# A 32-column projection on TensorE: three rounded passes in one corner of the array, or plain 32-bit products in four quarters of its columns

## What is computed

```python
D_MODEL = 1024; SEQ = 512; N_SSD_HEADS = 32; CHUNK = 128
...
zxbcdt = u @ w_in                       # u: (512, 1024), normed tokens
z, xbc, dt = jnp.split(zxbcdt, [D_INNER, D_INNER + D_XBC], axis=-1)   # dt: (512, 32)
xbc = jax.nn.silu(causal_depthwise_conv(xbc, conv_w, conv_b))
...
dt = jax.nn.softplus(dt + dt_bias)
a = -jnp.exp(a_log)
y = ssd_chunked(xh, dt, a, bm, cm)      # decays are exp of running sums of dt * a
```

## Time and profile before

| | |
|---|---|
| median of 3 runs | 1150.98 us (1150.7 to 1151.34) |
| profiled execution, its own time | 1151.16 us |
| its span | 1149.4 us |
| mean granted TensorE clock | 0.999 |
| TensorE (PE) busy | 1141.1 us, 99% of the span |
| VectorE (DVE) busy | 684.4 us, 60% |
| ScalarE (ACT) busy | 523.9 us, 46% |
| GpSimd (POOL) busy | 32.8 us, 3% |
| DMA queue of SyncE (q1) | 32.1% of 16 engines' span |

### The profile page before, as it was taken

One profiled execution on the slowest core, in us unless ns is written; L12 is line 12 of the kernel. 1 busy time (PEld: TensorE's weight loads), 2 busy tenths in 40 slices (PEclk: granted clock), 3 DMA queues, 4 the chain that ended last, 5 costly groups with the idle time before them and its releaser, 6 DMA issues.

```text
span 1149.4 us, 14668 instructions
## 1 busy us (share of the span) xinstructions
PE 1141.1 (99%) x5734; PEld 956.9 (83%) x5734; DVE 684.4 (60%) x783; ACT 523.9 (46%) x614; POOL 32.8 (3%) x87
## 2 busy tenths in 40 slices
PE   9999999999999999999999999999999999999998
PEld 8888888888788898888888888899888888888886
DVE  5678778888943865565555412487655565562124
ACT  5667676767523644444344211465444344342213
POOL 6000001000000000000000000000000000000000
PEclk9999999999999999999999999999999999999999
DMA  8243444443222323332322332512222323323321
GB/s 271 75 130 129 128 129 129 128 129 129 74 94 90 110 75 117 102 104 80 108 94 88 110 110 92 183 37 74 92 90 93 109 79 103 109 76 111 106 74 74
DMA packets 85246, 121.74 MB, mean 106 GB/s; under 512 B 4167, under 2 KB 71215, under 8 KB 85200
## 3 DMA queue, kind: packets, MB, share of 16 engines
q1 hardware_dynamic: 85018, 121.02, 32.1%
q10 hardware_dynamic: 182, 0.07, 0.0%
HBM read 118.92 MB, written 2.16 MB: 105 GB/s over the span
## 4 chain that ended last, share of the span: by engine, by line
PE 97%; DVE 2%; ACT 0%; issue 0%; POOL 0%; DVEq 0%; POOLq 0%; ACTq 0%
PE bank L994 28%; PE bank L300 18%; PE bank L302 18%; PE bank L301 18%; PE bank L497 6%; PE bank L777 2%; PE bank L786 1%; PE bank L414 1%; PE bank L709 1%; PE bank L736 1%; PE bank L1170 0%; DVE w_lo L270 0%; PE bank L764 0%; PE bank L437 0%; PE bank L432 0%; PE bank L1185 0%
## 5 line engine op out<-in xcount | busy, mean ns | idle before, releaser
L300 PE MATMUL bank<-h_hi,w_hi 128*128 128x512 f32 x928 | 364.1, 392 | 0.0
L302 PE MATMUL bank<-h_hi,w_lo 128*128 128x512 f32 x928 | 361.3, 389 | 0.0
L301 PE MATMUL bank<-h_lo,w_hi 128*128 128x512 f32 x928 | 361.1, 389 | 0.0
L270 DVE TENSOR_TENSOR w_lo<-raw,w_hi 128x2048 fp32r<-128x2048 f32 x90 | 206.2, 2291 | 219.7 <-ACT w_hi L265 219.7
L516 DVE SCALAR_TENSOR_TENSOR tmp<-bank,par,tmp 128x511 f32<-128x511 f32 (+2 forms) x248 | 184.7, 747 | 135.3 <-ACT tmp L507 122.4
L265 ACT ACTIVATE w_hi<-raw 128x2048 fp32r<-128x2048 f32 x90 | 171.5, 1906 | 152.5 <-PE bank L994 152.3
L302 PEld LDWEIGHTS bank<-h_hi,w_lo 128*128 128x128 f32 x928 | 174.2, 188 | 36.6
L301 PEld LDWEIGHTS bank<-h_lo,w_hi 128*128 128x128 f32 x928 | 174.3, 188 | 36.3 <-issue 0.7
L300 PEld LDWEIGHTS bank<-h_hi,w_hi 128*128 128x128 f32 x928 | 174.2, 188 | 36.4 <-issue 0.7
L507 ACT ACTIVATE tmp<-bank,par 128x512 f32<-128x512 f32 x112 | 86.3, 775 | 229.4 <-PE bank L302 209.5
L994 PE MATMUL bank<-w_hi,act_hi 128*128 128x512 f32 x348 | 107.2, 389 | 0.0
(11 more groups left out here) (193 smaller groups left out, 1035.9 us busy)
## 6 DMA issues: line engine op xcount, KB each, us to landing
raw<-in_ffn_w_up SPq DMA_DIRECT2D x44, 1024.0 KB, 5.1
raw<-in_ffn_w_down SPq DMA_DIRECT2D x22, 1024.0 KB, 5.0
raw<-in_ssd_w_in SPq DMA_DIRECT2D x19, 1024.0 KB, 5.5
decay<-ac_dram SPq DMA_DIRECT2D x16, 512.0 KB, 4.3
raw<-in_ssd_w_out SPq DMA_DIRECT2D x8, 1024.0 KB, 4.9
from_start<-ac_dram SPq DMA_DIRECT2D x32, 128.0 KB, 4.0
xres<-in_x SPq DMA_DIRECT2D x4, 512.0 KB, 5.7
result<-xres SPq DMA_DIRECT2D x3, 512.0 KB, 2.6
```

The lines of the kernel that those rows point to most:

```text
L270: dve.tensor_tensor(lo[:], raw[n % 2][:], hi[:].bitcast(F32), ALU.subtract).then_inc(lo_ready, 1)
L300: pe.matmul(dst, wh, xh, start=first, stop=False, **kw)
L301: pe.matmul(dst, wh, xl, start=False, stop=False, **kw)
L302: return pe.matmul(dst, wl, xh, start=False, stop=last, **kw)
```

## The change

The weights of the projection are no longer split. Each of the 8 contraction blocks `k` gives two plain 32-bit products, one with `h_hi` and one with `h_lo`, both read as fp32. Block `k` goes to quarter `k % 4` of the array's columns, and so to 32 of the 128 partitions of bank 7: two blocks in each quarter. The result is four partial sums stacked on 128 partitions. ScalarE copies all 128 rows. Where a 32 by 32 identity turned each chunk, a product with `fold` (128 by 32, four identities on top of each other) now turns it and adds the four partial sums at once. `fold` is built by GpSimd with three additions of slices of the identity, behind the masks that TensorE waits for at the start and ahead of the pooling windows.

```diff
-            wdt_hi = sb("wdt_hi", [P, DB, HEADS], F32R, scope=scope)
-            wdt_lo = sb("wdt_lo", [P, DB, HEADS], F32R, scope=scope)
+        fold = sb("fold", [P, HEADS])
...
         def dt_feat_act(act):
             act.wait_ge(dt_mm, 1)
-            act.activation(sq[0:HEADS, :], bank[0:HEADS, 7, :], ACT.Copy).then_inc(dt_feat_ready, 1)
+            act.activation(sq[:, :], bank[:, 7, :], ACT.Copy).then_inc(dt_feat_ready, 1)
...
-        def dt_split_act(act):
-            act.wait_ge(wdt_in, 16)
-            act.activation(wdt_hi[:], wdt_raw[:], ACT.Copy).then_inc(wdt_hi_ready, 1)
-
-        def dt_split_dve(dve):
-            dve.wait_ge(wdt_hi_ready, 1)
-            dve.tensor_tensor(wdt_lo[:], wdt_raw[:], wdt_hi[:].bitcast(F32), ALU.subtract).then_inc(wdt_ready, 1)
+        QUARTERS = P // HEADS
 
         def dt_product_pe(pe):
-            pe.wait_ge(wdt_ready, 1)
-            for k in range(DB):
-                mm = three_passes(pe, bank[0:HEADS, 7, :], wdt_hi[:, k, :], wdt_lo[:, k, :], h_hi[:, k, :],
-                                  h_lo[:, k, :], k == 0, k == DB - 1)
+            pe.wait_ge(wdt_in, 16)
+            for r in range(DB // QUARTERS):
+                for turn, part in enumerate((h_hi, h_lo)):
+                    for q in range(QUARTERS):
+                        k = r * QUARTERS + q
+                        mm = pe.matmul(bank[q * HEADS:(q + 1) * HEADS, 7, :], wdt_raw[:, k, :], part[:, k, :].bitcast(F32),
+                                       start=r == 0 and turn == 0, stop=r == DB // QUARTERS - 1 and turn == 1,
+                                       tile_position=(0, q * HEADS))
             mm.then_inc(dt_mm, 1)
 
         def dt_transpose_pe(pe):
             pe.wait_ge(dt_feat_ready, 1)
+            pe.wait_ge(fold_ready, 1)
             for c in range(NCH):
-                mm = pe.transpose(bank[:, 7, c * HEADS:(c + 1) * HEADS], sq[0:HEADS, cs(c)], ident[0:HEADS, 0:HEADS])
+                mm = pe.matmul(bank[:, 7, c * HEADS:(c + 1) * HEADS], sq[:, cs(c)], fold[:, :], start=True, stop=True)
             mm.then_inc(dt_T, 1)
...
             pool.wait_ge(consts, 4)
+            step(pool.tensor_tensor(fold[:, :], ident[:, 0:HEADS], ident[:, HEADS:2 * HEADS], ALU.add))
+            step(pool.tensor_tensor(fold[:, :], fold[:, :], ident[:, 2 * HEADS:3 * HEADS], ALU.add))
+            pool.tensor_tensor(fold[:, :], fold[:, :], ident[:, 3 * HEADS:], ALU.add).then_inc(fold_ready, 1)
...
-            dt_split_act(act)
...
-            dt_split_dve(dve)
```

More of the change, by code:

```diff
@@ L195, in hybrid_trunk @@
         x_sq, x_rms, x_rr, xn_ready = sem("x_sq"), sem("x_rms"), sem("x_rr"), sem("xn_ready")
+        fold_ready = sem("fold_ready")
         pre_spread, pre_kept, xn_half = sem("pre_spread"), sem("pre_kept"), sem("xn_half")
@@ L200, in hybrid_trunk @@
                                                                 sem("half_scaled"), sem("half_out"))
-        wdt_in, wdt_hi_ready, wdt_ready = sem("wdt_in"), sem("wdt_hi_ready"), sem("wdt_ready")
+        wdt_in = sem("wdt_in")
         dt_feat_ready, dt_T = sem("dt_feat_ready"), sem("dt_T")
```

## The result

The changed kernel takes 1157.05 us (1156.89 to 1157.78, 6 runs) against 1150.89 us before (6 runs): ratio 1.0057, 95% interval 1.0047 to 1.0067. It is 6.2 us slower, where 1.4 us faster was forecast. The profiled span is 1155.4 us, for 1149.4.

What follows compares the result with a forecast made beforehand. TensorE was taken to bound the kernel, busy 1141.1 of 1149.4 us. Product -1.76 and transposes +0.34 gave -1.4 us, from 1151.16 to 1149.7, set to 1149.6 for the runs' median; range 1148.8 to 1150.2.

Steps and rivals of the forecast that it cites:

- the product: The dt product on TensorE: 3.77 us in place of 5.53, 1.76 less.
- the switches: Price for changing column width around the dt product: together 0.35 us, on top of 3.42 us of streaming.
- eight slots: The dt product's 32 pieces run four side by side, in 8 slots of 0.4275 us: 3.42 us.
- strict program order: Rival: dt pieces start strictly in list order, only neighbours overlap, 17 slots, 7.62 us; kernel 1153.4; chance 0.07.
- two at a time: Rival: only two dt pieces run at once, 16 slots, 7.19 us with switches; kernel 1153.0; chance 0.08.
- the transposes: Folding products between blocks 4 and 5: 1.35 us for 1.01, so +0.34, range 0 to +0.5.
- what lies beside: Splits on ACT and DVE, copy of 128 rows, three POOL additions: no effect on the end; the copy starts earlier.
- what is late next: Inputs TensorE needs after the change: block 4 has 1.7 us of slack, dt_sums_pe 3.1; block 8 is tightest.
- the tight place at block 8: Block 8 waits for taps ending at 69.42, TensorE starts at 69.48; both sides were to move together.
- The sum: Whole kernel: -1.76 for the product and +0.34 for the transposes give -1.4 us, so 1149.6; chance 0.70.

Runs made afterwards that it cites:

- e2: The changed kernel with fold allocated in the gap behind wdt_raw, so that no other tile moves: 1149.14 us, ratio 0.9984 to the kernel before.
- e1: The kernel before with only an unused tile of 32 columns (128 bytes per partition) at fold's place: 1158.91 us, ratio 1.0068.
- e4: The kernel before with 32 unused columns ahead of its first tile, so that every tile moves by 128 bytes: 1150.47 us, ratio 0.9999.
- e5: The kernel before with 32 unused columns ahead of act_hi and act_lo alone: 1156.55 us, ratio 1.005.
- w32: e2 with 8 unused columns (32 bytes) ahead of raw0, so w_hi and act_hi move together and part from h_hi: 1165.69 us, ratio 1.0126.

## Why the prediction was wrong

**Right: the product.** Forecast 3.77 us with the switches, measured 3.57 (36.89 to 40.46), and 0.11 more for the first weight load behind it (40.46 to 40.80 is 0.34 for 0.23). The way in costs 0.09: the last product of line 497 starts 0.21 us ahead of the first dt product (36.68 to 36.89), where before two such products took 0.23 (37.43 to 37.66). Together 3.77. Before, then after:

```profile
37.43 0.40 PE L497 MATMUL bank<-h_hi,w_lo 128*128 128x256 f32 x2
```

```profile
36.68 0.28 PE L497 MATMUL bank<-h_hi,w_lo 128*128 128x256 f32 x1
```

There are eight slots with four pieces each, as line 786 had suggested with two. The rivals of strict program order (7.62 us) and of two at a time (7.19) fall. The Trainium skill ("TensorE: Matmul & The Clock Gate", Part 3, What overlaps and what doesn't) says that MATMULs never pass one another. The trace speaks against it if the two pieces of a product stand next to each other in the list, as the prediction took them to: then the second piece of a quarter starts 0.43 us behind the first pieces of the three others, which stand after it in the list. No row names the quarter of a piece, so the order of the pieces in the list is not shown.

**Right: the transposes.** Forecast 1.35 us from the last product of block 4 to the second of block 5. Measured 47.20 - 45.85 = 1.35. That the sum is exact is luck: the second of the 8 pieces starts 0.03 us behind the first and not 0.11, and the way out from the last piece (46.78) is 0.42 us and not 0.35.

**Right: what lies beside, and what is late next.** No wait was added, and the tight place at block 8 moved with PE: the taps now end at 67.24, and PE starts at 67.29. The copy to `sq` begins at 41.49, directly behind the silu that waits for taps, as said:

```profile
40.95 0.64 ACT L551 ACTIVATE xbc<-tmp 128x512 f32<-128x512 f32 x1 [2.45 <-DVE tmp L516]
41.49 0.58 ACT L566 ACTIVATE sq<-bank 128x512 f32<-128x512 f32 x1
```

The dt stretch as a whole went from 11.76 to 10.31 us, with the way in from 11.76 to 10.40: 1.36 less, and 1.4 was forecast. In the whole program this sum is confirmed by e2: 1149.14 measured, 1149.6 forecast.

**Wrong: "So around the change every us that leaves or enters PE's list should move the end by the same amount".** The sum priced instructions and waits, and took the durations of all instructions that were not edited as fixed. The diff also added a tile in the middle of the allocations. I followed `fold` only as work on POOL and as a semaphore. That its 128 bytes move the tiles behind it against those ahead of it was not a step of the prediction, and none of the rivals was this. e1 shows that this alone costs 8 us, e2 that the change without it has none of the loss, and the table that the measured 1157 is the value of a misfit of 128 bytes. A rival "the unedited products change their speed" with 1440 products and 0.0055 us would have given +7.9 - 1.4 = +6.5, near to what came. Nothing in the trace of before gave this price, since its fp32r products of 512 tokens with full-width weights all fit; but the starts that lie whole multiples of 256 apart, and the gap of 8 columns in front of the `wf` tiles, stood in the code and could have made me ask.

The trace of before also held a sign that addresses matter, in the dt products themselves. Each block's weights are 128 bytes wide, so from block to block their misfit runs through 0, 128, 256 and 384 bytes. The 24 distances between their starts add up to 5.53 us (37.66 to 43.19 in the earlier trace rows), 0.230 us each; the 23 distances of block 4 right behind them add up to 5.22 (43.19 to 48.41 in the earlier trace rows), 0.227 each. The prediction rounded both to 0.23. Taken one by one, the distances run from 224 to 239 ns and repeat every four blocks: from 229, 226, 236 for the first block to 235, 228, 232 for the third. In e1, whose pad moves these weights by 128 bytes, the same series stands one block earlier; in e4 and e5, where they don't move against `h_hi`, it stands as before. For weights of 32 columns the period is thus 512 bytes and not 256.

Open: what in the chip collides. The runs show that it belongs to the pair of weights and moving data, and that for full-width weights and 512 tokens it is gone again at 256 and at 512 bytes. That the weight load reads the memory while another product's moving data is read, and that the two disturb each other depending on their addresses, fits this. No run separates it from other causes.

## What to carry to other kernels

A new tile is part of a change: list which tiles move against which when it is allocated, and put small late additions behind everything, in a hole, or fill them up to 256 bytes (most of TensorE's time in this program goes to products of 512 tokens; at line 497, with 256 tokens, the misfit was no loss). When a kernel gets slower without a new wait, compare the mean duration of the most frequent instructions that nobody edited; 6 ns on 389 was the whole result. Products in different quarters of the columns run side by side here, so plain 32-bit products of 32 columns cost less than three rounded passes when four of them run at once, and more than twice as much when they don't.

## What the hardware showed that I had not expected

By the mean distance between starts in the timelines, a MATMUL of 512 tokens in fp32r streams in 0.227 us when weights and moving data start at the same place within 256 bytes, and in 0.232 to 0.234 us when they are 32 to 128 bytes apart. At 192 bytes the loss in the whole program was 2.9 us, for 8 to 9 at the smaller misfits. Moving both operands together by 128 bytes changed nothing measurable (1150.47 us). A product of 256 tokens took 0.120 us with a fit and 0.118 us at 32 bytes (e2 and w32). With weights of 32 columns the distances changed from block to block in steps of 128 bytes and repeated after 512, not after 256 (before and e1).
